# From the third expert on, each expert's w2 is loaded ahead of the w1 of the expert after next

## The reference

```python
def clamped_swiglu(h):
    x_glu = jnp.minimum(h[..., :D_FF], SWIGLU_LIMIT)
    x_lin = jnp.clip(h[..., D_FF:], -SWIGLU_LIMIT, SWIGLU_LIMIT)
    return x_glu * jax.nn.sigmoid(SWIGLU_ALPHA * x_glu) * (x_lin + 1.0)
...
    logits = (x @ router_w + router_b).astype(jnp.float32)
    top_vals, top_idx = lax.top_k(logits, TOP_K)
    gates = jax.nn.softmax(top_vals, axis=-1).astype(x.dtype)
...
        h = x_pad[tok] @ w1[e] + b1[e]
        return clamped_swiglu(h) @ w2[e] + b2[e]
```

## Time and profile before

| | us |
|---|---|
| median of 3 runs | 1155.74 (1154.76 to 1158.33) |
| the profiled execution's time | 1155.93 |
| its span in the trace | 1154.1 |
| PE busy | 1062.9 (92%) |
| DVE busy | 274.5 (24%) |
| ACT busy | 162.2 (14%) |
| share of the chain that ended last | PE 54%, DMA 39% |
| moved by DMA | 429.85 MB, mean 372 GB/s |

### The profile page before, as it was taken

How to read it: one execution, slowest core, us unless ns; L and a number is a source line. 1 busy time by engine, 2 the same in 40 slices (tenths; PEclk the granted TensorE clock), 3 DMA queues, 4 the chain that set the end, 5 groups by cost and what they waited for, 6 DMA issues and landing times.

```text
span 1154.1 us, 13351 instructions
## 1 busy us (share of the span) xinstructions
PE 1062.9 (92%) x4855; PEld 412.6 (36%) x4856; DVE 274.5 (24%) x717; ACT 162.2 (14%) x314; POOL 49.9 (4%) x90
## 2 busy tenths in 40 slices
PE   4996997999999899999998898998999999999996
PEld 3763545333333233333332233333333333333332
DVE  2999536111111111111111111111111111111112
ACT  3006221011111011111111111111111001111112
POOL 0100000000000000000000000000000000000000
PEclk9997997899999999999999899999999999999999
DMA  9835526599999978999999999999999999999994
GB/s 310 233 155 208 218 93 223 220 429 429 426 426 426 429 323 353 428 428 426 427 429 427 426 430 427 426 429 427 427 426 428 427 417 408 422 427 427 429 427 202
DMA packets 44026, 429.85 MB, mean 372 GB/s; under 512 B 6239, under 2 KB 13815, under 8 KB 19412
## 3 DMA queue, kind: packets, MB, share of 16 engines
q1 hardware_dynamic: 40540, 421.10, 88.0%
q0 software_dynamic: 3328, 8.17, 1.8%
q10 hardware_dynamic: 144, 0.39, 0.1%
HBM read 430.30 MB, written 4.62 MB: 377 GB/s over the span
## 4 chain that ended last, share of the span: by engine, by line
PE 54%; DMA 39%; DVE 4%; ACT 1%; issue 1%; SPq 1%; POOLq 0%; DVEq 0%; POOL 0%; ACTq 0%
DMA W<-in_w_dram 35%; PE PS L921 18%; PE PS L942 17%; DMA WB<-in_w_dram 4%; PE PS L675 3%; PE PS L642 3%; PE PS L789 2%; PE PS L638 2%; PE PS L692 2%; PE PS L913 1%; PE PS L631 1%; PE PS L683 1%; DMA WA<-in_state_conv_dram 1%; PE PS L613 1%; DVE WA L1009 1%
## 5 line engine op out<-in xcount | busy, mean ns | idle before, releaser
L942 PE MATMUL PS<-W,XT 128*64 128x512 f32 x1056 | 256.9, 631 | 43.6 <-DMA W<-in_w_dram 39.1
L921 PE MATMUL PS<-WB,X 128*64 128x512 f32 x1088 | 237.7, 594 | 2.4 <-DMA WB<-in_w_dram 2.4
L921 PE MATMUL PS<-WA,X 128*64 128x512 f32 x1024 | 224.9, 596 | 1.9 <-DMA WA<-in_w_dram 1.9
L1228 DVE TENSOR_SCALAR X<-PS 128x512 f32<-128x512 f32 x33 | 22.8, 692 | 590.6 <-PE PS L921 590.6
L942 PEld LDWEIGHTS PS<-W,XT 128*64 128x64 f32 x1056 | 77.1, 144 | 175.3 <-issue 128.7
L921 PEld LDWEIGHTS PS<-WB,X 128*64 128x64 f32 x1088 | 76.4, 137 | 162.5 <-issue 157.7
L921 PEld LDWEIGHTS PS<-WA,X 128*64 128x64 f32 x1024 | 72.1, 137 | 154.3 <-issue 150.6
L584 ACT ACTIVATE X<-X 128x512 f32<-128x512 f32 x33 | 20.8, 630 | 467.4 <-DVE X L1228 467.4
L1215 DVE TENSOR_TENSOR X<-PS,par 128x512 f32<-128x512 f32 x34 | 23.5, 692 | 199.9 <-PE PS L631 199.9
L642 PE MATMUL PS<-XT 64*128 64x512 f32 x272 | 67.8, 616 | 0.0
L591 ACT COPY XT<-PS 128x512 f32<-128x512 f32 x33 | 19.4, 587 | 309.1 <-PE PS L942 309.1
(11 more groups left out here) (235 smaller groups left out, 575.4 us busy)
## 6 DMA issues: line engine op xcount, KB each, us to landing
WA<-in_w_dram SPq DMA_DIRECT2D x64, 2048.0 KB, 25.4
WB<-in_w_dram SPq DMA_DIRECT2D x64, 2048.0 KB, 25.6
W<-in_w_dram SPq DMA_DIRECT2D x64, 2048.0 KB, 23.3
WB<-in_w_in_dram SPq DMA_DIRECT2D x5, 1024.0 KB, 12.0
WB<-in_w_in_dram SPq DMA_DIRECT2D x1, 2048.0 KB, 14.7
W<-in_w_out_dram SPq DMA_DIRECT2D x2, 1024.0 KB, 11.4
W<-in_w_out_dram SPq DMA_DIRECT2D x1, 2048.0 KB, 7.8
h_rows<-M POOLq DMA_DIRECT2D x3, 512.0 KB, 7.4
```

Of the source, the lines that this page charges most:

```text
L921: last = mm(PS[64 * n:64 * n + 64, s, :], xTe[:, o:o + SLOTS], w1buf[u][:, c, q:q + 512], start=False, stop=(c == 3 and k == 1))
L942: last = mm(PS[64 * n:64 * n + 64, MIX, :], hT[:, s, h, :], w2buf[:, 4 * h + s, 512 * n:512 * n + 512], start=(s == 0 and h == 0), stop=(s ...
```

## The change

`SWITCH` goes from 24 to 2. Experts 0 and 1 still use the loop; expert 2 has the mixed order, and experts 3 to 29 issue w2 first, where before only 25 to 29 did. What is loaded, into which buffer and behind which semaphore is as before. The programs of PE, DVE, ACT and POOL are the same.

```diff
-SWITCH = 24
+SWITCH = 2
```

## The result

The changed kernel takes 1163.87 us (median of 4 runs, 1163.59 to 1163.97) where the kernel before takes 1155.87 (4 runs): a ratio of 1.0066, with a 95% interval of 1.0048 to 1.0083. It is 8.0 us slower; 8.2 was forecast.

What follows compares the result with a forecast made beforehand. From about expert 5 the stream of weights was taken to set the pace, counted from its last restart. Later restart +9.12, slower first chunk +0.4, expert 24's turn -1.3: +8.2 on 1155.93, so 1164.1 us, range 1159.5 to 1169.5.

Steps and rivals of the forecast that it cites:

- The pace: Stream of weights: 4.984 us per chunk, gathers of tokens included, for 137 chunks after the restart.
- The rival of a faster stream with w2 first: Chunks 4.89 us apart throughout would give 1151.2 us; it decides at 4.92; chance 9%.
- The holes at experts 2 and 3: Stream idles 5.2 us at expert 2's mixed turn, 1.6 at expert 3's; the 6.8 vanish at expert 7, not added.
- the gap at expert 7: Empty queue at expert 7's two-block turn, from about 435.6; first issue at 445.33, 9.12 us later than before.
- PE's lead: Without stalls for w2, PE begins expert 8 at 450.37 instead of 458.93, 8.56 us ahead.
- The restart: After expert 7, the first chunk, now w2, lands slower than w1's 7.7 us: +0.4, between 0 and 0.9.
- a margin of 2.1: w1(7)c3 lands at 405.7 and PE needs it at 407.8: the tightest chunk, not late by 2.1 us.
- The turn of expert 24: The old mixed turn's shallow gap goes, as the queue is now full: -1.3 us, between -0.6 and -2.6.
- the prediction's second sum: Whole time as 445.33 + 8.1 + 137 x 4.984 + 0.3 + 26.1 + 1.8 = 1164.4 us.
- the rival of the later restart: Dearer early gaps make w1(7)c3 late and PE lose its lead at expert 7: +16.8, 1172.7 us; chance 9%.
- The clock: Rival: PE's clock back from 0.97 to 1.00 between 438 and 943 gains 15 us, giving 1141; chance 2%.

Runs made afterwards that it cites:

- w1 first from 7 on: Mixed turn at expert 2, w2 first for experts 3 to 6, w1 first from 7 to 23, end as in the kernel before: 1152.02 us, ratio 0.9967.
- the one almost without the early hole: Kernel before with the mixed turn at expert 4, w2 first at 5 and 6, w1 first from 7 to 23, same end: 1148.03 us, ratio 0.9933.
- the run without any such turn: Kernel before with w1 first for every expert, so without the switch at 24: 1171.16 us, ratio 1.0136.
- the switch at 14: Kernel before with SWITCH = 14 in place of 24, so w2 first from expert 14 on: 1156.26 us, ratio 1.0005.

## Why the prediction was right

**The pace.** Right. From w2(8)c0 (444.28 + 8.0 = 452.3) to w1(31)c3 are 137 chunks in 683.6 us, 4.990 each. The rival of a faster stream with w2 first is out: it needed 4.92.

**The holes at experts 2 and 3.** There, and as long as worked out. By landings the first is 5.0 us, where 5.2 was forecast: w1(4)c0 lands at 282.8 (267.19 + 15.6) and w2(3)c0 at 292.8 (284.88 + 7.9), and the chunk itself takes 4.98 of the 10.0 between. By bytes the window from 280 to 295 lacks more, (428 - 253) / 428 x 15 = 6.1 us. Expert 3's chunk took 8.0 to land. That the holes vanish in the gap at expert 7 follows from the sum below, which leaves nothing over for them. The experiments add that they count as soon as that gap is closed: w1 first from 7 on is 3.7 us under the kernel before (935.3 of span from the first issue) and the one almost without the early hole is 8.5 under it (930.5), 4.8 us between them, with expert 7's issue at the same moment in both (212.5 behind the first).

**PE's lead.** Expert 8 begins 235.40 us after the first issue (449.46 - 214.06) where it began 243.81 after (458.93 - 215.12 by the earlier trace rows): 8.41 against the 8.56 forecast. Taken where the sum uses it, at the release of w2 that SP waits for, the lead is 8.55: 453.89 - 215.12 = 238.77 before, 230.22 after. So SP's restart came 9.13 later, and 9.12 was worked out. The condition for it held: w1(7)c3 landed at 404.0 (issued 370.6, 33.4 to landing), and PE needed it at 406.8 (396.32 + 10.5), 2.8 us later. The forecast had a margin of 2.1, but its chain of landings is not quite its own spacing: 320.5 + 5 x 4.98 is 345.4 and not 345.8, the later ones are 0.4 to 0.6 late as well, and put right the margin is 2.6. The sum uses only the lead.

**The restart.** +0.3 (8.0 against 7.7) where +0.4 was taken. The Trainium skill's fit that the prediction quotes (DMA: Bandwidth & Descriptors, Anatomy of one DMA) is given there for DMAs that GpSimd issues. For these, issued by SP, its estimate of 6.8 us is low by 0.9 to 1.5: 7.7 to 8.3 were measured.

**The turn of expert 24.** The one term that was mis-sized: -1.3 was taken, between -0.6 and -2.6. The stream behind the restart is only 0.5 us shorter (683.6 against 684.1), and the run without any such turn shows the same 4.993 us per chunk as the kernel before. So the bytes missing between 943 and 990 cost nothing that can be told from the scatter of the pace. I had taken the slower last 35 chunks for the gap's doing, and that run has them as slow without a gap (5.01 us each).

**What made the total fit so well.** The mechanism was right; that the total fits to 0.2 us is in part luck. From the first issue the span grew by 9.13 + 0.3 - 0.5 = 8.9 (measured 8.96), 0.8 above the forecast 8.2. Against that, what lies ahead of it was 1.06 shorter in this execution. That is no larger than such shifts in other kernels: the one with SP's code written out and the order as before had its first issue at 217.23, 2.1 later. With one profile of each kernel it isn't shown whether the change has a part in it. The medians, 8.0 apart, hold such shifts too. And the prediction's second sum, 1164.4, has a term of +0.3 without a source; without it, it gives 1164.1 like the first.

**The later restart and the clock.** In the changed kernel PE had no stall for weights in experts 6 and 7, and kept its lead, so the rival of the later restart didn't come about. The clock did come back, 1.00 for 0.97 between 447 and 943, and gave nothing; the switch at 14 shows the same, with a mean clock of 0.981 for 0.969 in the kernel before and no time gained. The Trainium skill's rule (TensorE: Matmul & The Clock Gate, Why this matters for your kernels) holds for the clock here, and the DMA share of 1.01 says why the time doesn't follow.

## What to carry to other kernels

When two loads share one queue, the order is a choice of which wait the queue stands behind: putting the later-released buffer first starves the stream by the difference of the two releases, but only where the queue is short at that moment. Behind a long queue (experts 14 or 24 here) the same swap is free, and at the end it was worth 15 us. So choose the order turn by turn: earn the consumer's lead while the queue is deep enough, and give the earliest-released load the front where a long stay of the consumer (the expert with two blocks) will empty it. Count a stream-bound kernel's time from its last empty queue, and don't add earlier holes that a later one swallows.

## What was not expected of the hardware

Fewer bytes in a window need not mean lost time: 943 to 990 moved 404 GB/s where 427 to 428 is full, 2.6 us by bytes, and the landings of the chunks behind it show none of it (5.02 us each, and 5.01 in the kernel without that gap). And the same instructions ahead of the experts end at different times: the first issue of expert 0's turn lay between 214.0 and 217.4 us in these profiles, one of each kernel. That is about the spread of the kernel before from run to run (1154.05 to 1158.05), and it is why the sums above start from there.
